# Seven block products in place of eight for the gate and up products of a macaron FFN

## The reference, cut to what matters

```
def _swiglu(h, w_gate, w_up, w_down):
    return (jax.nn.silu(h @ w_gate) * (h @ w_up)) @ w_down

x = x + 1/2 * _swiglu(_rmsnorm(x, norm), w_gate, w_up, w_down)     # twice
```

## Time and profile before

| | us |
|---|---|
| median of 3 runs | 2910.88 |
| lowest, highest | 2910.38, 2914.92 |
| the profiled execution, its own time | 2911.83 |
| its span in the profile | 2910.0 |
| PE busy | 2836.9 (97%) |
| DVE busy | 1268.8 (44%) |
| ACT busy | 582.8 (20%) |
| POOL busy | 1232.4 (42%) |

### The profile page before, as it was taken

How to read it: one execution, slowest core, us unless ns; L and a number is a source line. 1 busy time by engine, 2 the same in 40 slices (tenths; PEclk the granted TensorE clock), 3 DMA queues, 4 the chain that set the end, 5 groups by cost and what they waited for, 6 DMA issues and landing times.

```text
span 2910.0 us, 38225 instructions
## 1 busy us (share of the span) xinstructions
PE 2836.9 (97%) x14892; PEld 2380.5 (82%) x14892; DVE 1268.8 (44%) x1203; ACT 582.8 (20%) x903; POOL 1232.4 (42%) x654
## 2 busy tenths in 40 slices
PE   7999999999999999999999999999999999999996
PEld 5888888888888888877988878887888888888885
DVE  5331332234556524017787866532344312331344
ACT  3100100002100122125666641112321100000011
POOL 3334334434444446644556563432134344334331
PEclk9999999999999999999999999999999999999998
DMA  3111111112322224323212213320011111111111
GB/s 131 49 51 47 47 50 50 45 49 84 114 101 90 105 96 143 130 91 74 55 34 54 49 59 130 105 76 29 15 51 44 50 51 43 50 51 43 51 42 74
DMA packets 99115, 196.61 MB, mean 68 GB/s; under 512 B 14288, under 2 KB 56400, under 8 KB 98792
## 3 DMA queue, kind: packets, MB, share of 16 engines
q1 hardware_dynamic: 78032, 138.06, 15.9%
q10 hardware_dynamic: 21016, 57.59, 5.2%
HBM read 160.93 MB, written 34.67 MB: 67 GB/s over the span
## 4 chain that ended last, share of the span: by engine, by line
PE 87%; issue 5%; POOL 3%; DVE 3%; ACT 1%; DMA 1%; ACTq 0%; POOLq 0%; DVEq 0%; SPq 0%
PE G L663 26%; PE G L665 26%; PE G L664 26%; PE G L892 2%; PE G L1061 1%; POOL AL L596 1%; PE G L1084 1%; PE G L789 1%; PE G L795 1%; DMA zm<-zml_d 0%; DVE ylo L1967 0%; POOL rkb L571 0%; POOL Ys L556 0%; DVE nt_a L1541 0%; PE G L729 0%
## 5 line engine op out<-in xcount | busy, mean ns | idle before, releaser
L622 POOL TENSOR_TENSOR whi<-raw,zero 128x1024 fp32r<-128x1024 f32 (+1 forms) x213 | 398.3, 1870 | 1407.0 <-PE G L665 1403.7
L663 PE MATMUL G<-hhi,whi 128*128 128x512 f32 x2288 | 894.2, 391 | 16.9 <-DVE hlo L1547 16.9
L665 PE MATMUL G<-hhi,wlo 128*128 128x512 f32 x2288 | 891.7, 390 | 0.0
L664 PE MATMUL G<-hlo,whi 128*128 128x512 f32 x2288 | 891.7, 390 | 0.0
L625 POOL TENSOR_TENSOR wlo<-raw,whi 128x1024 fp32r<-128x1024 f32 (+1 forms) x213 | 518.1, 2433 | 16.7
L663 PEld LDWEIGHTS G<-hhi,whi 128*128 128x128 f32 x2288 | 430.1, 188 | 108.9 <-issue 13.0
L665 PEld LDWEIGHTS G<-hhi,wlo 128*128 128x128 f32 x2288 | 430.1, 188 | 89.7
L664 PEld LDWEIGHTS G<-hlo,whi 128*128 128x128 f32 x2288 | 430.2, 188 | 89.3 <-issue 0.7
L663 PE MATMUL G<-ahi,whi 128*128 128x512 f32 x960 | 374.2, 390 | 2.7 <-DVEq L439 2.7
L665 PE MATMUL G<-ahi,wlo 128*128 128x512 f32 x960 | 373.7, 389 | 0.0
L664 PE MATMUL G<-alo,whi 128*128 128x512 f32 x960 | 373.7, 389 | 0.0
(11 more groups left out here) (327 smaller groups left out, 3168.5 us busy)
## 6 DMA issues: line engine op xcount, KB each, us to landing
raw<-in_wg SPq DMA_DIRECT2D x44, 512.0 KB, 3.5
raw<-in_wu SPq DMA_DIRECT2D x44, 512.0 KB, 3.5
raw<-in_wd SPq DMA_DIRECT2D x32, 512.0 KB, 3.5
raw<-in_ml_in SPq DMA_DIRECT2D x16, 512.0 KB, 3.5
zml_d<-po ACTq DMA_DIRECT2D x16, 512.0 KB, 2.7
gates_d<-po ACTq DMA_DIRECT2D x16, 512.0 KB, 2.7
zm<-zml_d SPq DMA_DIRECT2D x8, 1024.0 KB, 5.7
sg<-gates_d ACTq DMA_DIRECT2D x16, 512.0 KB, 4.8
```

What stands on the lines that cost most here:

```text
L622: nc.gpsimd.tensor_tensor(hi, raw[:, k, 0:w], zero[:].to_broadcast([P, w]), ALU.add).then_inc(hi_made, 1)
L663: nc.tensor.matmul(dst, wh, hi, start=start, stop=False)
L664: nc.tensor.matmul(dst, wh, lo, start=False, stop=False)
L665: return nc.tensor.matmul(dst, wl, hi, start=False, stop=stop)
```

## The change

The gate unit and the up unit of one inner tile are taken as a 2 by 2 matrix of blocks (gate or up, by first or second four input tiles), the input as a 2 by 2 matrix (first or second four input tiles, by token half). Their product is made with seven block products instead of eight. A block product is 4 tiles by 3 matmuls of 512 columns. The first 3 inner tiles of an FFN stay plain (`PLAIN`), the other 19 (`FAST`) take the new form.

- **Input sums.** During the plain tiles ACT scales `xT` in place by the norm's gain (`scale_tile`), DVE forms three differences and a fourth per tile and their lo parts (`tile_sums`, 32 operations of 512 columns), ACT their hi parts (`tile_hi`). They take the room of `ahi`, `alo` and half of `xT`; `xT` is read back from DRAM (`reload`) during the down products.
- **Weight sums.** Per fast pair POOL waits for both halves of `raw`, forms four sums (S1 to S4) of 512 columns and seven lo parts of 512 columns, and then frees both halves (`split_made` by 2). ACT makes the seven hi parts (`weight_hi`). Each of the seven hi and lo slots is single.
- **Combination.** ACT copies two products out of PSUM, DVE runs ten operations per pair (`fast_pair`): V, g0, U3, c12, c21 read PSUM; g1, c22, m, a0, a1 have both inputs in SBUF, all 512 columns but m, which has 1024. Silu stays on ACT.
- **Activations.** Each inner tile is stored to DRAM (`a_d`) by SP and is loaded again, two tiles at a time, in each of two passes of the down products. A down unit is two inner tiles by four output tiles, so 22 units instead of 24. ACT and DVE split 128 by 2048 activations for each (`dh`, `dl`). Pass one makes output tiles 0 to 3, pass two 4 to 7; the last two units of pass two run together, output tile by output tile.

```diff
-FF_PARTS = (8, 8, 6)
+FFK = FFC // 2
+PLAIN = 3
+FAST = FFC - PLAIN
...
+            with sp.Fori(2, FAST - 1) as q:
+                pair(q)
+                sp.wait_ge(*st_dve.at("a1", q + (c.fast - 2)))
+                store_a(q + (PLAIN - 2))
...
+        def weight_sums(q, u0):
...
+            for n in range(2):
+                u = u0 + 2 * PLAIN + n
+                pool.wait_ge(raw_in[u % 2], (q + (u // 2 + 1)) * 16)
+            pool.wait_ge(*wh_act.at("h6", it - 1))
+            tt(S1, a21, a22, ALU.add).then_inc(*wl_pool.sig("S1"))
+            pool.wait_ge(*wl_pool.at("S1", it))
+            tt(S2, S1, a11, ALU.subtract).then_inc(*wl_pool.sig("S2"))
+            tt(S3, a11, a21, ALU.subtract).then_inc(*wl_pool.sig("S3"))
+            pool.wait_ge(*wl_pool.at("S2", it))
+            tt(S4, a12, S2, ALU.subtract).then_inc(*wl_pool.sig("S4"))
+            pool.wait_ge(*wl_pool.at("S4", it))
+            for n, (x, (hi, lo)) in enumerate(zip((a11, S2, S1, a12, S3, S4, a22), fast_slots(k))):
+                pool.wait_ge(*wh_act.at(f"h{n + 1}", it))
+                ins = tt(lo, x, hi.bitcast(F32), ALU.subtract)
+                if n < 6:
+                    ins.then_inc(*wl_pool.sig(f"l{n + 1}"))
+                else:
+                    ins.then_inc(split_made, 2)
...
+            block(0, a_, *tokens(0, 0), True).then_inc(*st_pe.sig("P1"))
...
+            block(1, b_, T2[:, 0], T2[:, 1], True).then_inc(*st_pe.sig("P6"))
...
+            block(2, c_, T1[:, 0], T1[:, 1], True).then_inc(*st_pe.sig("P5"))
...
+            block(3, a_, *tokens(4, 0), False).then_inc(*st_pe.sig("P2"))
...
+            block(4, b_, T3[:, 0], T3[:, 1], False).then_inc(*st_pe.sig("P7"))
...
+            pe.wait_ge(*st_act.at("s5", it))
+            block(5, c_, *tokens(4, 1), False).then_inc(*st_pe.sig("P3"))
...
+            block(6, d_, T4[:, :, HALF:T], T4[:, :, 0:HALF], True).then_inc(unit_used, 2)
...
+            ready(20, 20)
+            ready(21, 21)
+            for o in range(4):
...
+            activation(s1c[:], a_, ACT.Copy).then_inc(*st_act.sig("s1"))
+            if more:
+                weight_hi(q + 1, 1, k)
+            act.wait_ge(*st_pe.at("P5", it))
+            act.wait_ge(*st_dve.at("a1", it - 1))
+            activation(s5c[:], c_, ACT.Copy).then_inc(*st_act.sig("s5"))
...
+                act.wait_ge(d_in[v % 2], (turn + turns) * 16)
+                if not isinstance(at, int) or at >= 2:
+                    act.wait_ge(unit_used, at + (first - 1 + credit))
...
```

More of the change, by code:

```diff
@@ L498, in mixers_io, with store_a, ffn_up, plain @@
             sp.wait_ge(*f_dve.at("S0s", LAST))
+        c = Count()
+        def store_a(p):
+            sp.dma_start(a_d[p], s0[:]).then_inc(a_out, 16)
+        def ffn_up(names, u0, load):
+            free = PLAIN_AT[c.ffn] + credit
+            def plain(u):
+                load((u0 + u) % 2, names[u % 2], u // 2, u0 + u)
+            def pair(q):
+                for n, name in enumerate(names):
+                    u = u0 + 2 * PLAIN + n
+                    load(u % 2, name, q + PLAIN, q * 2 + u)
+            for u in range(2 * PLAIN - 1):
+                plain(u)
+            for p in range(PLAIN):
+                sp.wait_ge(dve_free, free + p + 1)
+                store_a(p)
+                if p == 0:
+                    plain(2 * PLAIN - 1)
+                if p < 2:
+                    pair(p)
+            with sp.Fori(2, FAST - 1) as q:
+                pair(q)
+                sp.wait_ge(*st_dve.at("a1", q + (c.fast - 2)))
+                store_a(q + (PLAIN - 2))
+            pair(FAST - 1)
+            sp.wait_ge(a_out, (c.ffn * FFC + FFC - 3) * 16)
+            sp.wait_ge(*t_dve.at("d4", c.tile + 3))
+            sp.dma_start(draw0[:], a_d[0:2].rearrange("k p t -> p k t")).then_inc(d_in[0], 16)
+            sp.wait_ge(*st_dve.at("a1", c.fast + FAST - 3))
+            store_a(FFC - 3)
@@ new lines, in ffn_down, with pair @@
+        def ffn_down(name, u0, load):
+            last, lo = c.fast + FAST - 1, c.ffn * 2 * FFK
+            parked = a["x"] if c.ffn == 0 else x_park
+            def pair(v):
+                j = v % FFK
+                dst = draw[v % 2] if v else draw0
+                sp.dma_start(dst[:], a_d[2 * j:2 * j + 2].rearrange("k p t -> p k t")).then_inc(d_in[v % 2], 16)
+            for v in range(2):
+                load((u0 + v) % 2, name, v, u0 + v)
+            sp.wait_ge(*st_dve.at("a1", last - 1))
+            store_a(FFC - 2)
+            sp.wait_ge(a_out, (c.ffn * FFC + FFC - 1) * 16)
+            sp.wait_ge(*st_pe.at("P7", last))
+            pair(1)
+            sp.wait_ge(*st_dve.at("a1", last))
+            store_a(FFC - 1)
+            sp.wait_ge(a_out, (c.ffn * FFC + FFC) * 16)
+            sp.wait_ge(unit_used, u0 + credit)
+            for v in range(2, 2 * FFK):
+                load((u0 + v) % 2, name, v, u0 + v)
+                sp.wait_ge(*d_dve.at("lo", lo + v - 2))
+                pair(v)
+                if v in reload:
+                    k = reload.index(v)
+                    sp.dma_start(xT[:, k, :], parked[:, k, :]).then_inc(xc_in[k], 16)
+            next_ffn(c)
@@ L735, in norm_chunk @@
             pe.wait_ge(*nh_dve.at(f"l{t % 2}", c.norm + t // 2))
-        def ffn(nt):
[L738 to L759, removed]
@@ new lines, in ffn @@
+        def ffn(nt):
+            k = c.unit % 2
+            for r in range(PLAIN):
+                act_bank(c.act + r)
+                unit_ready(c.unit + 2 * r)
+                product(bank_act(c.act + r), (c.unit + 2 * r) % 2, range(KD), hhi, hlo,
+                        norm_chunk if r == 0 else None).then_inc(unit_used, 1)
+                if r == 0:
+                    norm(nt, T)
+                    c.norm += 4
+                dve_bank(c.dve + r)
+                unit_ready(c.unit + 2 * r + 1)
+                product(bank_dve(c.dve + r), (c.unit + 2 * r + 1) % 2, range(KD), hhi, hlo).then_inc(unit_used, 1)
+            c.advance(unit=2 * PLAIN, act=PLAIN, dve=PLAIN)
+            held = (act_free, c.act + credit), (dve_free, c.dve + credit)
+            with pe.Fori(0, FAST // 2) as i:
+                for s in range(2):
+                    fast_pair(i * 2 + s, s, k, held[s])
+            fast_pair(FAST - 1, 0, k, held[0])
+            c.advance(unit=2 * FAST, act=1, dve=1)
+            down()
+            next_ffn(c)
@@ L1179, in mem_norm, with weight_hi @@
                 activation(memhi[:, k, :], memh[:, k % 2, :], ACT.Copy).then_inc(*mh_act.sig(f"c{k % 2}"))
[L1181 to L1193, removed]
+        def weight_hi(q, n, k):
+            it = q + c.fast
+            a11, a12, a21, a22 = (raw[:, m, h * HALF:(h + 1) * HALF] for m in (k, 1 - k) for h in range(2))
+            x = (a11, Sw[:, 1, :], Sw[:, 0, :], a12, Sw[:, 2, :], Sw[:, 3, :], a22)[n - 1]
+            if n == 1:
+                for m in range(2):
+                    u = c.unit + m
+                    act.wait_ge(raw_in[u % 2], (q + (u // 2 + 1)) * 16)
+            name = {2: "S2", 3: "S1", 5: "S3", 6: "S4"}.get(n)
+            if name:
+                act.wait_ge(*wl_pool.at(name, it))
+            if n < 7:
+                act.wait_ge(*st_pe.at(PROD[n - 1], it - 1))
+            else:
+                act.wait_ge(unit_used, q * 2 + (c.unit + credit))
+            activation(fast_slots(k)[n - 1][0], x, ACT.Copy).then_inc(*wh_act.sig(f"h{n}"))
@@ new lines, in plain_silu, with fast_pair @@
+        def plain_silu(r):
+            act.wait_ge(act_free, c.act + r + 1 + credit)
+            activation(s0[:], s0[:], ACT.Silu).then_inc(f_silu, 1)
+        def fast_pair(q, s, k, more=True, down=None):
+            it = q + c.fast
+            a_, b_, c_, d_ = fast_banks(s)
+            act.wait_ge(*st_pe.at("P1", it))
+            act.wait_ge(*st_dve.at("U3", it - 1))
+            activation(s1c[:], a_, ACT.Copy).then_inc(*st_act.sig("s1"))
[4 more added lines that the diff above has]
+            activation(s5c[:], c_, ACT.Copy).then_inc(*st_act.sig("s5"))
+            if more:
+                for n in range(2, 7):
+                    weight_hi(q + 1, n, k)
+            else:
+                act.wait_ge(*st_pe.at("P6", it))
+                down(0, 0)
+            act.wait_ge(*st_dve.at("g1", it))
+            activation(s0[:], s0[:], ACT.Silu).then_inc(*st_act.sig("silu"))
+            if more:
+                weight_hi(q + 1, 7, k)
+            else:
+                act.wait_ge(*st_pe.at("P5", it))
+                down(1, 1)
@@ new lines, in ffn, with down @@
+        def ffn(own, gain, hi, nms, park=False):
+            norm_root(nms, nrf[:])
+            k = c.unit % 2
+            act.wait_ge(*nh_dve.at("l1", c.norm - 1))
+            if c.ffn:
+                act.wait_ge(store, 2 * KD * 16)
+            scale_tile(0, own)
+            plain_silu(0)
+            scale_tile(1, own)
+            tile_hi(0)
+            scale_tile(2, own)
+            tile_hi(1)
+            plain_silu(1)
```

(104 more changed lines are left out.)

305 lines of the change are left out of this document (269 added, 36 removed).

## The result

The changed kernel takes 2980.24 us (median; 2978.93 to 2985.0 in 4 runs) against 2911.82 for the kernel before, a ratio of 1.0236 with a 95% interval of 1.0219 to 1.0254. It is slower by 68 us where 2900 was forecast with a range up to 2955. Its profiled span is 2977.4, 67.4 over the span of before.

What follows compares the result with a forecast made beforehand. PE, busy 97%, was taken as the bound, with POOL's load-and-work series (21.5 us per pair) replacing it. Each FFN: -13.9 + 8.5 = -5.4; both -10.8 from 2911.83 gives 2901.0, median 2900, range 2862 to 2955.

Steps and rivals of the forecast that it cites:

- The mechanism: Fast pairs: load and POOL's work, in series, replace PE as bound; period 21.5 us against PE's 19.04.
- PE's wait for s5: Fast pair: PE's sixth product waits for ACT's copy, held behind h1 until the next landing; free while period over about 21.
- PE's wait for l1: Start of each fast pair: PE waits for POOL's lo part, ready 6.9 us after the landing.
- The plain tiles, the steady down units and the tail: Rest of each FFN: no added time; only the plain tiles had an upper end, 5 us.
- both loads: Fast pair's raw weights: 4.7 us, upper end 5.7, plus 0.1 until POOL starts; the store behind them not counted.
- Meetings with DVE: POOL's stretch of a fast pair: four meetings of 0.34 and one of 0.85, 2.2 us per pair.
- The start of the down products: After the last fast pair: weights, `dl` and activations ready in time; 0, upper end 3 us.
- The first fast pair: After F, when PE's last plain unit is done: `raw` free at F + 3.2, pair 1 landed at F + 8.1.
- The last two units: End of down products: PE waits 6.8 us, plus 1.7 for its fallen clock; 8.5 per FFN, ends 4 and 10.
- Rival 1: Fast pairs: each meeting costs POOL DVE's whole operation, 4.0 for 2.2; period 23.3, 2950 us; chance 0.27 including slow loads.
- Rival 4: Fast pairs: PE's new waits lower its clock, so no PE saving; one more us per pair, 2934 us; chance 0.08.

Runs made afterwards that it cites:

- e4_raw_free_sooner: On the changed kernel POOL makes the seventh lo part, the last reader of raw, fifth, so the next loads start two operations sooner: 2839.78 us.
- e1_store_first: On the changed kernel SP issues the activation's store before the next pair's loads, in the fast loop and at its end: 2929.21 us.

## Why the prediction was wrong, point by point

- **The mechanism held.** The bound moved from PE to the series of load and POOL's work; PE's wait for s5 and the one long gap per FFN stand where they were named. PE's wait for l1 does not: PE came to it late from the gap before the sixth product and the slower matmuls behind that. The plain tiles, the steady down units and the tail cost nothing visible. That the series sets the period is shown by e4_raw_free_sooner, which takes two operations out of it. The period came out as 23.1 and not 21.5, and at 3.4 us for a tenth that turns a small gain into a loss.
- **The term that failed most: both loads.** The step says that the store "is issued behind both loads and so isn't counted". The loads took 5.97 to POOL's start where 4.8 was summed. `memx`'s 4.7 was the right row for the loads by themselves: with the store elsewhere they took 5.0. The row had no store 0.6 us behind it. 34 x 1.17 = 40 us of the 79 between 2901 and 2980.
- **Meetings with DVE** were 2.7 and not 2.2, and POOL's stretch with them 0.35 longer than summed up: 34 x 0.35 = 12 us. The 0.34 came from operations in the mixers; in this pair three of the four meetings of 512 columns take 0.45 and one 0.23, and m takes 0.97 and not 0.85.
- **The start of the down products**, taken as 0 with 3 as the upper end, cost 7.9 in the first FFN: 6.1 of waits and 1.8 of slower matmuls behind them. The step followed weights and `dl` and not SP's queue: the store of pair 17 stood behind the wait for two down weight loads, so g0 of pair 18 started at 515.43 and U3 and c21, which free PSUM, stood behind g0 and the `dl` of 2.9 us that follows it. In e1_store_first PE's waits are gone, and the down products are 14 us shorter. By the rows of the changed kernel it is 15 us for both FFNs.
- **The first fast pair.** The second pair's loads were issued 5.8 after F and not 3.4. About 2.5 us per FFN: 5.
- **The last two units** were sized well: 6.94 plus 2.7 of slower matmuls, 9.7 against 8.5, 2 us for both FFNs. Pulling them apart gains only about half of that price.
- **Rival 1** has a slip: with a period of 23.3 each FFN is +25.2, so both give 2911.8 + 50.4 - 0.95 = 2961, and not 2950. With its right sum the rival lies outside the stated range, which ended at 2955. The measured period is near its 23.3, but 1.2 of the missing 1.6 are the loads, so its nearness says nothing for it. Nor does its row L556 show what was read from it: POOL's operation started at 1453.91, ahead of the DVE operation at 1454.07.
- **Rival 4's clock** did fall, to 0.95 in the fast stretch, and was absorbed as argued: POOL goes from the landing to the free `raw` without a pause, so the period is that of loads and POOL, and the slower matmuls took the place of PE's wait for l1.

These terms sum to 40 + 12 + 15 + 5 + 2 = 74 of the 79 us, and 1.7 are in the attention stretch. What the last 3 are was not found.

## What to carry to other kernels

Where a change takes work off the bound by giving more to another engine, sum the longest loop that no longer passes through the bound, buffer by buffer: here one pair of load buffers, held until the last of eleven operations, made a load and a work stretch add up that had overlapped. The order in which that engine reads the buffer then counts as much as the amount of its work: the last reader of the raw data should come as early as its wait allows. And a transfer that is "behind" another in a queue was here neither free for the one ahead nor for those who waited for it.

## What was not expected of the hardware

- A 512 KB store issued 0.6 us behind two 512 KB loads on SP's queue lengthens them: from first issue to POOL's start 5.99 us on average against 5.00 with the store issued ahead. With the store 1.7 us behind it was 5.26, with 4.0 us 5.05 (e4_raw_free_sooner).
- PE's granted clock fell to 0.95 over the fast stretch of the changed kernel, in which PE waited 2.2 us for s5 once per pair on average (at most 3.3). Behind some twenty of the 34 waits matmuls started 0.43 us apart in place of 0.23. With no such waits, in e4_raw_free_sooner, the clock was 1.00.
- At a granted clock of 1.00, matmuls of the same shape started 0.2333 us apart with weights from `whx` and `wlx`, and 0.2267 with weights from `whi` and `wlo`. No run here shows the cause.
